# Two norms between attention layers: squares, roots, sums, scalings and halves of the four token tiles issued in another order, with one weight unit split between them

## What is computed

```python
def rmsnorm(x, g):
    xf = x.astype(jnp.float32)
    y = xf * lax.rsqrt(jnp.mean(xf * xf, axis=-1, keepdims=True) + EPS)
    return (y * g.astype(jnp.float32)).astype(x.dtype)

for i in range(DEPTH):
    u = rmsnorm(x, norm_pre[i])
    y = nsa_mixer(u, ...) if i % 2 == 0 else diff_mixer(u, ...)   # ends in o @ w_out
    x = x + rmsnorm(y, norm_post[i])
```

## Time and profile before

| | |
|---|---|
| median of three runs | 1475.75 us (1475.18 to 1480.19) |
| the profiled execution | 1474.46 us, with a span of 1472.6 us |
| mean granted TensorE clock | 0.992 of full |
| busy: PE, POOL, ACT, DVE | 1377.1, 781.1, 712.9, 618.9 us |
| instructions in the trace | 20918 |

### The profile page before, as it was taken

How to read it: one execution, slowest core, us unless ns; L and a number is a source line. 1 busy time by engine, 2 the same in 40 slices (tenths; PEclk the granted TensorE clock), 3 DMA queues, 4 the chain that set the end, 5 groups by cost and what they waited for, 6 DMA issues and landing times.

```text
span 1472.6 us, 20918 instructions
## 1 busy us (share of the span) xinstructions
PE 1377.1 (94%) x7818; PEld 1119.0 (76%) x7818; DVE 618.9 (42%) x1602; ACT 712.9 (48%) x1525; POOL 781.1 (53%) x729
## 2 busy tenths in 40 slices
PE   6999999999989999988999999899999999999997
PEld 5877777777878888766778888777878787777785
DVE  3321067787151001695230012971441145887143
ACT  4242258888333223674433233972443254887252
POOL 5362356666454344385553443786456324566652
PEclk9999999999999999999999999999999999999999
DMA  6232310000434232111443223324224221001521
GB/s 237 86 116 89 111 58 30 30 30 1 158 98 158 87 115 86 58 59 55 164 125 121 109 86 115 144 74 171 101 86 186 97 104 58 2 1 59 186 86 58
DMA packets 27876, 139.57 MB, mean 95 GB/s; under 512 B 3328, under 2 KB 3712, under 8 KB 16128
## 3 DMA queue, kind: packets, MB, share of 16 engines
q1 hardware_dynamic: 14112, 98.57, 18.6%
q10 hardware_dynamic: 13664, 39.66, 7.8%
HBM read 129.83 MB, written 8.39 MB: 94 GB/s over the span
## 4 chain that ended last, share of the span: by engine, by line
PE 70%; POOL 11%; DVE 9%; ACT 5%; issue 3%; DMA 1%; ACTq 0%; POOLq 0%; SPq 0%; DVEq 0%
PE psum L391 57%; POOL w_lo L346 3%; PE psum L1174 3%; POOL w_free L1333 3%; PE psum L1155 3%; PE psum L1129 2%; DVE w_free L1223 2%; DVE u_lo L1236 2%; PE psum L872 1%; ACT w_hi L337 1%; POOL split L1350 1%; PE psum L1142 1%; DVE arena L741 1%; DMA w_raw<-in_weights 1%; ACT u_hi L1276 1%
## 5 line engine op out<-in xcount | busy, mean ns | idle before, releaser
L346 POOL TENSOR_TENSOR w_lo<-w_raw,w_hi 128x2048 fp32r<-128x2048 f32 (+2 forms) x118 | 426.8, 3631 | 440.2 <-ACT w_hi L337 439.4
L391 PE MATMUL psum<-u_lo,w_hi 128*128 128x512 f32 (+1 forms) x712 | 279.7, 393 | 3.9 <-DVE split L505 1.6
L391 PE MATMUL psum<-u_hi,w_hi 128*128 128x512 f32 (+1 forms) x712 | 277.3, 389 | 0.0
L391 PE MATMUL psum<-u_hi,w_lo 128*128 128x512 f32 (+1 forms) x712 | 277.3, 389 | 0.0
L337 ACT ACTIVATE w_hi<-w_raw 128x2048 fp32r<-128x2048 f32 (+1 forms) x93 | 172.6, 1858 | 154.3 <-DMA w_raw<-in_weights 103.1
L391 PE MATMUL psum<-w_hi,split 128*128 128x512 f32 x608 | 195.7, 394 | 6.0 <-POOL w_lo L346 2.6
L789 ACT ACTIVATE w_free<-w_free,neg_max 128x256 f32<-128x256 f32 (+3 forms) x320 | 183.6, 580 | 14.6 <-DVE neg_max L911 7.3
L391 PEld LDWEIGHTS psum<-u_lo,w_hi 128*128 128x128 f32 (+1 forms) x712 | 133.2, 187 | 33.9 <-issue 4.3
L391 PEld LDWEIGHTS psum<-u_hi,w_hi 128*128 128x128 f32 (+1 forms) x712 | 133.1, 187 | 28.7
L391 PEld LDWEIGHTS psum<-u_hi,w_lo 128*128 128x128 f32 (+1 forms) x712 | 133.2, 187 | 27.6
L391 PE MATMUL psum<-w_hi,u_lo 128*128 128x512 f32 (+2 forms) x352 | 135.2, 384 | 10.4 <-DVE u_lo L747 7.6
(11 more groups left out here) (190 smaller groups left out, 2124.1 us busy)
## 6 DMA issues: line engine op xcount, KB each, us to landing
w_raw<-in_weights SPq DMA_DIRECT2D x90, 1024.0 KB, 4.8
x<-x_scratch ACTq DMA_DIRECT2D x12, 512.0 KB, 6.7
gain<-in_gains ACTq DMA_DIRECT2D x10, 512.0 KB, 4.5
gain<-in_strips ACTq DMA_DIRECT2D x16, 256.0 KB, 2.9
spare<-in_strips ACTq DMA_DIRECT2D x16, 256.0 KB, 2.8
x_scratch<-x ACTq DMA_DIRECT2D x16, 256.0 KB, 4.1
gain<-in_near ACTq DMA_DIRECT2D x8, 512.0 KB, 4.1
w_raw<-in_near ACTq DMA_DIRECT2D x8, 512.0 KB, 3.7
```

The costliest lines, as they stand in the source:

```text
L346: low = nc.gpsimd.tensor_tensor(w_lo[b][:, c], w_raw[b][:, c], w_hi[b][:, c].bitcast(F32), ALU.subtract)
L391: mm = nc.tensor.matmul(dst, lhs, rhs, start=(a == 0 and k == 0 and (wl, ul) == (0, 1)), stop=(a + 1 == u and k + 1 == nk and (wl, ul) == ...
```

## The change

It reorders the three bodies, splits the high part of the `late` unit into two halves that stand among the squares, and moves the four pieces of its low part up among the roots. No instruction's work is changed; two more are issued (one ACT copy of 128x2048 becomes two of 128x1024, at either place). PE's and SP's programs are the same.

```diff
@@ chain_scalar (ACT)
             split_next(act, name, 1, 0)
+            late = next_unit(RUNS[name], 1, 1)
             square_y(act, c, name, 1, 0)
+            split_high(act, late, 0, 2)
+            square_y(act, c, name, 1, 1)
             square_x(act, c, 0)
-            square_y(act, c, name, 1, 1)
+            split_high(act, late, 1, 2)
             square_y(act, c, name, 1, 2)
             square_x(act, c, 1)
             high_tile(act, c, 0)
             square_y(act, c, name, 1, 3)
-            split_next(act, name, 1, 1)
+            high_tile(act, c, 1)
             square_x(act, c, 2)
-            high_tile(act, c, 1)
+            high_tile(act, c, 2)
             square_x(act, c, 3)
-            high_tile(act, c, 2)
             high_tile(act, c, 3)
@@ chain_pool (GpSimd)
             split_low(pool, n + 2)
             root_y(pool, c, 0)
+            root_y(pool, c, 1)
             root_x(pool, c, 0)
-            root_y(pool, c, 1)
+            split_low(pool, n + 3, 0)
             root_y(pool, c, 2)
             root_x(pool, c, 1)
+            split_low(pool, n + 3, 1)
             root_y(pool, c, 3)
-            split_low(pool, n + 3, 0)
-            split_low(pool, n + 3, 1)
+            split_low(pool, n + 3, 2)
             root_x(pool, c, 2)
-            split_low(pool, n + 3, 2)
+            split_low(pool, n + 3, 3)
             root_x(pool, c, 3)
-            split_low(pool, n + 3, 3)
@@ chain_vector (DVE)
             take_y(dve, c, 1, 1)
+            add_y(dve, c, name, 1)
             norm_tile(dve, c, 0)
-            add_y(dve, c, name, 1)
             take_y(dve, c, 1, 2)
             low_tile(dve, c, 0)
             norm_tile(dve, c, 1)
             add_y(dve, c, name, 2)
+            low_tile(dve, c, 1)
             take_y(dve, c, 1, 3)
+            norm_tile(dve, c, 2)
             add_y(dve, c, name, 3)
-            low_tile(dve, c, 1)
-            norm_tile(dve, c, 2)
+            low_tile(dve, c, 2)
             norm_tile(dve, c, 3)
-            low_tile(dve, c, 2)
             low_tile(dve, c, 3)
```

## The result

The change is slower by 0.3%, outside the range that was forecast.

The account below looks back on a forecast made before the run. PE's products were taken to bound the kernel, so only PE's waits and slow clock at two places could change. One clock fall per place, 1.3 us each, added 2.6 to 1474.46: 1477.1 us, range 1472.5 to 1480.2.

Parts of the forecast that it names:

- Half 0 waits for its load: On ACT, the first half of the w_hi copy waits until its load lands at 411.54, then takes 1.06 us.
- x-power 0 inside add 1: On POOL, x-root 0's power would start during DVE's add 1 and end 0.43 us after it, at 416.06.
- piece 0 started 0.07 ahead of norm 0: The w_lo piece behind x-root 0 takes the SBUF port 0.05 us ahead of DVE's norm, which then takes 2.29 us.
- turn 0 after 2.12 of wait: PE's first turn at a place starts at 418.45, after a 2.1 us wait that it does not have today.
- Waits ahead of turns 2 and 3: PE would stand 2.2 us ahead of turn 2 and 1.6 us ahead of turn 3, at the first place.
- So at an even clock the place ends where it does now: Turn 3 at 433.85 against 433.88 today: 6.7 us of waits replace 4.2 us and the slow stretch.
- the norms did not win the port: Rival: norms 0 and 2 get the port before POOL's piece and take 1.28 us; 1470.5 us, 15 in 100.
- the waits did not vanish: Rival: all 5.9 us per place of PE's waits and slow clock go, giving 1462.7 us; 3 in 100.
- half 0's load was not late: Rival: the load lands 1 us later, delaying y-square 1; with two clock falls 4.0 us per place, 1482.5; 8 in 100.
- One fall per place: PE's clock falls once at each place: 1.7 us, 0.4 hidden in a wait, so 1.3 us per place.
- What is left is the clock: With the place's end unchanged at an even clock, only clock falls at the two places would cost: 1.3 us each.
- behind it come only products whose operands are ready: After turn 3, at 433.88 in the kernel before, PE's products would wait for no operands; no size given.

Follow-up runs that it names:

- the repeated run: The changed kernel measured once more, unaltered: median 1483.38 us, 1.0022 of the kernel before.
- the other order: Kernel before with y-square 1 ahead of x-square 0, whole w_hi copy behind x-square 1, adds 1 and 2 ahead of norms 0 and 1: 1476.1 us, ratio 0.9984.
- the later look: The changed kernel, unaltered, run again for a third trace: that execution took 1477.64 us.

## Why the prediction was wrong

**Right, step by step.** Half 0 waits for its load (forecast 2.07 us behind the first y-square, measured 2.02) and takes 1.06; y-square 1 right behind it; add 1 ahead of norm 0; x-power 0 inside add 1, 1.43 us long; piece 0 started 0.07 ahead of norm 0, which takes 2.28; turn 0 after 2.12 of wait for the 2.1 forecast. The page "SBUF — State Buffer" of the Trainium skill, section "Who interferes with whom", has the same contention, of a DVE instruction with two SBUF inputs against a GpSimd instruction that reads SBUF, and calls it an exclusive lock. The trace agrees in who waits; taken to the letter norm 0 would have ended 0.3 later, and the rows stand on the forecast's side (8.83 for 8.9). Waits ahead of turns 2 and 3 are 1.77 and 1.28 for 2.2 and 1.6: each is 0.3 to 0.4 short with the turn on time at an even clock, so PE arrives that much later than reckoned from 0.23 a product. The forecast's sum could have told: it has 6.7 us of waits end the place where 4.2 of waits and 1.7 of slow clock end it, 0.8 too much for the same work. The waits at an even clock measured 2.23, 0.27, 0.28, 1.78 and 1.29, 5.85 in all. "So at an even clock the place ends where it does now" is measured as 24.45 against 24.41. So the rivals fall: the norms did not win the port, the waits did not vanish, and half 0's load was not late (y-square 1 at 2.99 for 3.0).

**The size of the fall at a place.** One fall per place at 1.3 us was forecast. It is 1.0 where it comes (1.24 once), and at the second place it came in two of four traces. Two places so come to 1.0 to 2.3 (1.24 and 1.02 in the repeated run) for the 2.6 forecast, which was too much if anything.

**The step that failed** is the sentence "What is left is the clock", together with "behind it come only products whose operands are ready". The clock was counted at the two places alone, and everything behind turn 3 was taken as it is today. It isn't. In all four traces of the change the clock is low for 10.2 us in the differential attention, some 220 us behind the first place, in code with the same waits as before. That costs 2.5 to 2.8 us, more than both places. Places 1.0 to 2.3 and attention 2.6 give 3.6 to 4.9, and the means differ by 3.9.

The times bear this out as a steady loss: the fastest of the 22 executions of the change took 1477.64 us and has the fall in the attention in its trace, and 62 of the 119 executions of before took less.

That it isn't the order of the change as such is shown by the pair of shifts: 1.06 us of idle work in the kernel before brings the fall, 2.5 us of it in the change take it away, each without touching the order. Each has one trace, and only the times of the second agree. It is a matter of timing, but counted from the first place and not from the start of the program. The fall in the attention is also where the other order, 2.2 us shorter at each place, gave back 2.7 us.

**The base** was a second term that was mis-sized. The 2.6 us were added to 1474.46, one execution. Over the 119 of before the median is 1477.3 and the mean 1478.4. The eight that the change was compared with have a median of 1475.45. So of the 4.0 us by which the measured 1481.12 lies above the forecast, 1.0 is the base and 3.0 are the change's (5.7 measured, 2.6 forecast).

**The range** failed by the same step. Its upper end came from half 0's load, and no rival had the clock fall elsewhere. Scatter was taken from three runs, 1475.18 to 1480.19. The 119 executions of before go from 1473.6 to 1491.2; behind them stand falls that come in one trace and not in another. The first trace of the change has 2.6 us between 200 and 235, 2.0 between 1110 and 1140 and 1.5 between 1240 and 1260 on top of its steady losses; the third trace of before has 2.1 at the second of these, and the first trace of before has a fall at 978 that the others lack (all of them gain 0.3 to 0.7 there, from 970 to 1110). That is how two single traces come to differ by 10.7 us where the means differ by 3.9.

**What stays open.** Why the chip lowers the clock in the attention at some distances from the first place and not at others was not settled. Nor was it settled which falls near 122, 217, 978, 1130 and 1255 belong to a kernel and which to the execution: with one to four traces for each, only the one in the differential attention, the one at the first place and the one near 1100 are regular. What the untraced slow executions of before, up to 1491.2 us, have low is unknown. And the interval of the change's second measurement, 0.9998 to 1.0047, just takes in 1.

## What to carry to other kernels

Where PE waits in short pieces all along, the price of a change is not read at its place alone: list every stretch in which PE waits again and again, also where each wait is as short as 1.35 us, and put each into the range as won or lost. Moving work by a microsecond cost or won 2.5 us or more some 220 us later, so look for the rest of a difference by comparing the start of the same instruction in two traces, and judge a tuned order by several traces and not by one. Filling a wait with idle products paid some 2 us at the places, where it left 0.14 us or more of each wait over; in the attention, where it added 2.3 us of delay at full clock, it didn't pay.

## What the runs showed of the hardware

- The clock fell after waits of PE of 1.35 and 0.27 us near one another (at 661 of the change), and not after 2.23 us (ahead of 736.37 of the later look). The length of a single wait doesn't tell.
- The same code with the same waits had the fall when the delay had grown by 0.6 to 1.3 us or by -2.2 since the first place, and had none at -0.2 to 0.0, 3.1 and 3.7.
- 10.2 us at the lower level cost 2.5 to 2.8 us and not half of 10.2: there PE is busy 8.76 us of 10.20 at full clock and 10.04 at the lower, so part of the slower products goes into its waits.
- A POOL instruction queued behind the one that releases a DVE instruction gets the shared port first: the piece starts 0.04 us before the end that the power's row shows, the norm 0.07 us later and 1.0 us longer than alone. Moved one root further down, the same piece holds norm 1 instead (2.30 for 1.28).
